# Output projection: sums of squares from two products per tile instead of four, with a second GpSimd add ahead of them

## The reference, cut to what matters

```
mixed = jnp.concatenate([_rms(out_sb, sb_norm_g), _rms(out_lru, lru_norm_g)], axis=-1)
h = h + mixed @ w_out
h = h + _hier_moe(_rms(h, norm2_g), w_group, b_group, w_fine, b_fine, ...)
```

## Time and profile before

| what | value |
| --- | --- |
| median of 3 runs | 4551.26 us (4545.16 to 4552.74) |
| the profiled execution's own time | 4547.56 us |
| its span in the profile | 4545.7 us |
| TensorE busy over the span | 4254.8 us (94%) |
| VectorE, ScalarE, GpSimd busy | 2908.9, 2559.7, 571.9 us |
| mean granted clock of TensorE | 0.972 |

### The profile page before, as it was taken

How to read it: one execution, slowest core, us unless ns; L and a number is a source line. 1 busy time by engine, 2 the same in 40 slices (tenths; PEclk the granted TensorE clock), 3 DMA queues, 4 the chain that set the end, 5 groups by cost and what they waited for, 6 DMA issues and landing times. The chain is left out here.

```text
span 4545.7 us, 85984 instructions
## 1 busy us (share of the span) xinstructions
PE 4254.8 (94%) x28623; PEld 3186.5 (70%) x28625; DVE 2908.9 (64%) x3529; ACT 2559.7 (56%) x4010; POOL 571.9 (13%) x758
## 2 busy tenths in 40 slices
PE   6999979997998998999996999959999999999998
PEld 5888867775555555555554888847888788888886
DVE  3222246777998998998995444456666555555665
ACT  3222225555887887887885322335656555555665
POOL 0000002222000000000000000002233323222232
PEclk9999989998999999999998999979999999999999
DMA  4222231113012012011002433327666555555664
GB/s 135 99 102 106 86 123 46 65 55 119 16 37 64 16 37 64 16 39 54 6 6 90 149 129 129 124 94 254 226 232 219 211 204 201 190 192 191 235 248 143
DMA packets 279575, 540.02 MB, mean 119 GB/s; under 512 B 38320, under 2 KB 103856, under 8 KB 279344
## 3 DMA queue, kind: packets, MB, share of 16 engines
q1 hardware_dynamic: 228512, 410.49, 25.6%
q0 software_dynamic: 46224, 118.03, 7.5%
q10 hardware_dynamic: 4608, 8.39, 0.5%
HBM read 410.97 MB, written 176.16 MB: 129 GB/s over the span
## 5 line engine op out<-in xcount | busy, mean ns | idle before, releaser
L1036 DVE TENSOR_TENSOR_SCAN att_R<-att_stay,att_R 128x512 f32<-128x512 f32 x896 | 1058.9, 1261 | 27.4 <-ACT att_stay L976 25.4
L986 ACT ACTIVATE att_RT<-att_rt 128x512 f32<-128x512 f32 (+3 forms) x1152 | 585.8, 562 | 234.5 <-PE att_rt L927 204.3
L927 PEld LDWEIGHTS att_rt<-ident,att_R 64*128 64x128 f32 x8448 | 320.1, 139 | 373.2 <-issue 369.6
L976 ACT ACTIVATE att_stay<-att_z 128x1024 f32<-128x1024 f32 (+2 forms) x576 | 555.5, 965 | 25.7 <-PE att_z L914 24.0
L940 PE MATMUL att_out<-att_RT,att_dv 128*64 128x512 f32 (+3 forms) x2304 | 520.1, 572 | 0.1
L927 PE MATMUL att_rt<-ident,att_R 64*128 64x64 f32 x8448 | 384.2, 228 | 99.2 <-ACT att_RT L986 55.4
L1401 DVE TENSOR_TENSOR ew_lo<-ew_raw,ew_hi 128x1024 fp32r<-128x1024 f32 x384 | 444.0, 1218 | 22.0 <-ACT ew_hi L1394 13.6
L1394 ACT ACTIVATE ew_hi<-ew_raw 128x1024 fp32r<-128x1024 f32 x384 | 373.7, 1047 | 103.8 <-PE ex_down L1788 97.3
L243 PE MATMUL qkv_out<-qkv_u_hi,qkv_w_hi 128*128 128x512 f32 x768 | 310.3, 404 | 11.6 <-DVE qkv_u_lo L234 11.6
L243 PE MATMUL qkv_out<-qkv_u_hi,qkv_w_lo 128*128 128x512 f32 x768 | 302.2, 393 | 0.0
L243 PE MATMUL qkv_out<-qkv_u_lo,qkv_w_hi 128*128 128x512 f32 x768 | 300.2, 391 | 0.0
(11 more groups left out here) (260 smaller groups left out, 8105.6 us busy)
## 6 DMA issues: line engine op xcount, KB each, us to landing
ew_raw<-in_w_e_gate SPq DMA_DIRECT2D x32, 2048.0 KB, 9.3
ew_raw<-in_w_e_up SPq DMA_DIRECT2D x32, 2048.0 KB, 9.4
ew_raw<-in_w_e_down SPq DMA_DIRECT2D x32, 2048.0 KB, 9.2
qkv_x<-in_x SPq DMA_DIRECT2D x32, 512.0 KB, 5.0
lru_x<-in_x SPq DMA_DIRECT2D x32, 512.0 KB, 5.2
mix_raw<-s_mix_t SPq DMA_DIRECT2D x32, 512.0 KB, 4.2
mix_x<-in_x SPq DMA_DIRECT2D x32, 512.0 KB, 4.9
s_h<-mix_h SPq DMA_DIRECT2D x32, 512.0 KB, 3.7
```

What stands on the lines that cost most here:

```text
L927: last = nc.tensor.transpose(rt[half][:, h, qt, :], R[lanes, n % 3, h, qt, s * P:(s + 1) * P], k.ident[lanes, lanes])
L976: done = nc.scalar.activation(pair(stay[:, step % 4, :]), pair(z[step % 2][:]), ACT.Sigmoid, scale=-scale)
L986: nc.scalar.activation(RT[:, :, s, first:, half, :], rt[half][:, :, first:, :], ACT.Copy).then_inc(rt_copied[half], 1)
L1036: nc.vector.tensor_tensor_scan(R[:, n % 3, h, s, 0:width][:, ::-1], src[:, ::-1], src[:, ::-1], initial, ALU.mult, ALU.bypass).then_inc(sc ...
```

## The change

GpSimd adds once more. The two chunks of `sq2` that belong to one half are added into one chunk of a new tile `sq4`, so that a tile of 128 tokens has two chunks left, one per half. GpSimd waits for its own first add before that (`sq2_ready`), and a new semaphore `sq4_ready` tells TensorE that the second is done. TensorE then takes one product for each half, not two that accumulate, and waits for `sq4_ready`, not for `sq2_ready`. ScalarE's wait for `sq2_ready`, by which it may overwrite `sq`, stays as it was.

```diff
             sq2 = sb("mix_sq2", [P, 2, DC // 2, P])
+            sq4 = sb("mix_sq4", [P, 2, 2, P])
...
+            sq4_ready = sem("mix_sq4_ready")
...
                     nc.gpsimd.tensor_tensor(sq2[:, t % 2, :, :], pairs[:, :, 0, :], pairs[:, :, 1, :], ALU.add).then_inc(sq2_ready, 1)
+                    pool.wait_ge(sq2_ready, T + 3)
+                    halves = sq2[:, t % 2, :, :].rearrange("p (h two) s -> p h two s", two=2)
+                    nc.gpsimd.tensor_tensor(sq4[:, t % 2, :, :], halves[:, :, 0, :], halves[:, :, 1, :], ALU.add).then_inc(sq4_ready, 1)
...
-                    pe.wait_ge(sq2_ready, T + 3)
+                    pe.wait_ge(sq4_ready, T + 1)
                     pe.wait_ge(rms_ready, T + 1)
                     for half in range(2):
-                        for c in range(NP // 2):
-                            end = nc.tensor.matmul(sums[:, half:half + 1], sq2[:, t % 2, half * NP // 2 + c, :], k.ones[:],
-                                                   start=(c == 0), stop=(c == NP // 2 - 1))
+                        end = nc.tensor.matmul(sums[:, half:half + 1], sq4[:, t % 2, half, :], k.ones[:], start=True, stop=True)
```

## The result

The changed kernel takes 4509.83 us (median of 4 runs, 4508.54 to 4511.28), the kernel before 4548.21 (4 runs, 4544.67 to 4552.74). The ratio is 0.9915, with a 95% interval of 0.9898 to 0.9932. The forecast was 4511.3 us, a gain of 40.0 us; the medians differ by 38.4. The forecast started from 4551.26, 3.1 us above this median of the kernel before, so that the two absolute times lie as close as 1.5 us is in part luck; the gain, off by 1.6, is the fairer measure.

What follows compares the result with a forecast made beforehand. TensorE's own instruction stream was taken to set the time from the second of 32 tiles on. From 4551.26 us, 13.8 for removed pairs and 26.2 for clock falls (40.0 together) gave 4511.3 us, range 4503 to 4529.

Steps and rivals of the forecast that it cites:

- Step 1: TensorE's sums: four fewer pairs of load and matmul per tile, 0.445 us each tile, 13.8 us over 31 tiles.
- Step 2: TensorE's clock after the sums: stretch without a wide product shortened from 2.59 to 2.15 us, all 17 falls gone, 26.2 us.
- the straight line: Clock falls after the sums: interpolating by stretch length would leave 13 falls at 2.15 us; the prediction did not take it.
- B: Clock falls after the sums stay as frequent as they are; 4537.5 us; chance 0.11.
- C: Some clock falls after the sums stay, 4 to 12; 4517 to 4530 us; chance 0.08.
- Step 3: GpSimd's added 128x256 add per tile: 0.7 us plus 0.1 for the wait, hidden under a 10.1 us cover.
- the dear bound: Upper bound for GpSimd's new add, 1.28 us, with up to 0.67 more if slowed.
- Steps 4 and 5: TensorE's wait before the sums, now for the second add, costs nothing; no new wait elsewhere, u2 having 4 us spare.
- D: Falls depend on where in time small products stand, so more tiles are hit; with all 31, 4559.1 us; chance 0.03.
- E: Second add comes late, or four pairs at the sums cost as much as eight; 4551 or above; chance 0.02.

Runs made afterwards that it cites:

- sums moved: Kernel before with its four products per tile taken behind the tile's first 12 wide products, not beside the logits: 4523.13 us, ratio 0.9948.
- the series: Changed kernel's two products beside the logits against three, four, five and six per tile: 4509.8, 4514.9, 4549.0, 4559.8 and 4571.0 us.
- GpSimd's part alone: Changed kernel with second add and its wait kept, but TensorE taking four products from the first add's result: 4549.02 us, ratio 1.0005 to kernel before.
- five and six products: Changed kernel with a half's product repeated beside the logits, five or six per tile in place of two: 4559.8 and 4571.0 us.

## Why the prediction was right, step by step

**What bounds the kernel.** Right. TensorE's stream sets the time in this stage: pairs added or removed appear in the time at 0.10 to 0.11 us each per tile, and five more adds on GpSimd don't appear in the median.

**Step 1, the pairs.** The forecast was 0.445 us per tile and a tile of 14.27 us; it measured 0.45 and 14.26.

**Step 2, the clock.** The forecast was that all 17 falls go, for 26.2 us. None is left in the 31 tiles. The falls' price was shown by itself when the sums were moved: 23.4 us with no instruction taken away (from the ratio's interval, 16 to 31 us). The choice against the straight line between 0.79 and 2.59 us was right: the line would have left 13 falls at 2.15 us, and the series shows a jump between 2.38 and 2.59. But the argument for it, that half the tiles escape at 2.59 us and this length must be near the edge, was an inference ahead of any row of such a length, and the longer stretches don't bear it out: at 2.82 us 11 tiles of 31 still escape and at 3.04 us 7. That tiles escape does not by itself say that the edge is near. That the edge lies above 2.15 us was in part luck: had it been below, falls would have stayed, as in case B or C.

**Step 3, the add.** The forecast was 0.7 us plus 0.1 for the wait; it measured 0.738, and 2704.45 - 2703.07 - 1.30 = 0.08 between the adds. The cover was put at 10.1 us from the first add's end. It is 9.2 us from the second's. "Each us beyond it costs 31" was not tried; with 5.67 us of adds TensorE hardly waits on them. The prediction's "eight times as long as the dear bound" counts only 1.28 us; with the slowed 1.95 us that it names as well, it would be five times. It said that VectorE's work beside the new add has slack. With one add that holds, no tile of the changed kernel being longer than 14.28 us; with six the slack is used up in six tiles.

**Steps 4 and 5, the waits.** No new wait came. In the first tile the sums start at 2470.27, 0.4 us later than before, and the wait behind them took that up.

**The rivals.** B is out: there is no fall in the changed kernel from the second tile on. By the Trainium skill ("TensorE: Matmul & The Clock Gate", section "HAM oscillation — how this bites in real kernels") the cure for a falling clock is to leave no long idle gaps. No kernel here has such gaps after the second tile, yet the clock falls in four of them (the one before, GpSimd's part alone, five and six products) and not in the other six. The rule is not contradicted, but it doesn't cover this case. C is out with B. D, that it is where in time the small products stand which decides, is out as stated: a shorter stretch never had more falls, and the run with the sums moved has the kernel before's tile of 14.71 us and no fall. But time plays a part above the jump, since at 2.59 us tiles with the same instructions do or don't have a fall, and in a regular order. By the starts of successive sums, the kernel before has from the fourth tile on four long tiles (16.3 us) and three short ones (14.7 us) in every seven, never two short ones in a row, and so has GpSimd's part alone; with six products every fifth tile is a short one. What sets this order stays open. E is out: the sums are x4 and 0.45 us long.

**The rest of 1.3 us.** The spans differ by 38.7 us, the sum says 40.0. Most of it stands ahead of the second tile's sums. They start at 2500.48, 1.5 us later than the 2498.97 of the kernel before, as these timeline rows of the changed kernel show:

```profile
2492.46 0.80 PE L1247 MATMUL mix_out<-mix_w_hi,mix_hi 128*128 128x512 f32 x1 [5.08 <-DVE mix_w_lo L298]
...
2497.32 0.53 PE L1247 MATMUL mix_out<-mix_w_lo,mix_hi 128*128 128x512 f32 x1
2497.69 0.40 PE L1247 MATMUL mix_out<-mix_w_hi,mix_hi 128*128 128x512 f32 x1
```

The weights came later here: a wait of 5.1 us, not 3.9, ended 0.7 us later than in the kernel before (2491.74). And the slow products after it lasted until 2497.7, over 5.2 us, where those of the kernel before lasted 3.5 us, until 2495.25; at half the pace that is some 0.9 us more. In the traces taken that wait was 3.2 and 3.9 us in the two kernels without a second add and 4.6 to 7.0 us in the eight with it. Whether the add has a hand in it or the loads differ by chance from one execution to the next stays open; at 1 or 2 us it is below what the medians tell apart.

## What to carry to other kernels

When an engine is 100% busy, read the clock beside the share: here the same busy share held 17 falls of about 3.4 us at half speed, which cost 26 us. A group of small matmuls costs its own time and, where it makes a long enough run with the group beside it, a fall of the clock that wide products then pay for; putting wide products between two such groups (sums moved) removed the falls with no work saved. Before shortening such a group, look whether it adjoins another.

## What the runs showed that was not expected

The falls are not in proportion to the length of the stretch: by the traces 0 of 31 tiles at 2.15 and 2.38 us, 17 at 2.59, 20 at 2.82 and 24 at 3.04. So the third product of a tile cost 5 us in all, the fourth 34 (4549.0 - 4514.9).

A pair of load and matmul of one column costs 0.11 us in front of a wide product or another pair, and about 0.10 in front of the transposes (four in 0.39 us by the tiles' distance, 0.36 by the medians). A one-column product in fp32 is two such pairs and in fp32r with two columns one, at the same 0.11 us.
